# Latent attention: a turn, a spread row and a copy for each head, with the steps of the two heads interleaved

## The chip, the core and the metric

The kernel runs on one core of a Trainium2 chip. The core has TensorE (PE), which multiplies matrices and writes to PSUM; VectorE (DVE) and ScalarE (ACT), which read and write SBUF and PSUM; GpSimd (POOL), which in this kernel adds and multiplies in SBUF; and SyncE (SP), which here issues DMAs. Each has its own queue and takes its instructions in order; they wait for one another through semaphores. The metric is the device time of one execution in microseconds (us); lower is better.

## The reference

The whole reference is a model of two blocks of layers. The change touches one stage of it, the latent attention (MLA) of layer 0. Tokens are 256 of a context and 1024 of the sequence, 1280 in all; there are 8 heads, whose queries and keys have 64 + 32 (rotated) values and whose values have 64.

```python
q = to_heads(rmsnorm(cq, q_norm) @ w_uq, MLA_HEADS)
kv = to_heads(rmsnorm(ckv, kv_norm) @ w_ukv, MLA_HEADS)
...
def block_attention(q, k, v, scale):
    ...
    def one_block(qi):
        s = jnp.einsum('bhqd,bhkd->bhqk', qi, k).astype(jnp.float32) * scale
        p = jax.nn.softmax(s, axis=-1).astype(v.dtype)
        return jnp.einsum('bhqk,bhkd->bhqd', p, v)
...
a_lat = block_attention(qa_l, jnp.concatenate([ka_c, ka_l], axis=2), jnp.concatenate([va_c, va_l], axis=2), scale)
y_ctx = combine(block_attention(qa_c, ka_c, va_c, scale), h_c, mo_c, z_c, u_ctx.dtype)
```

Sequence queries see all 1280 keys, context queries see the 256 keys of the context. Everything is fp32.

## The kernel before

The stage is `mla_block`. Its first part (projections, norms, keys and values) is not touched. The part that the change touches is the attention loop at its end.

**Tiling.** A group is one pair of heads j (0 to 3) and one tile t of 128 query tokens. For each pair there are 8 full groups (t from 2 to 9, 10 tiles of 128 keys each) and then 2 small ones (t = 0 and 1, 2 key tiles each): 40 groups. A unit u is one head of one group, u = 2g + hh, where hh says head 0 or head 1 of the pair. Scores lie transposed: keys on partitions, queries along the row. Head 0 has PSUM banks 0 to 2 (`S[0]`), head 1 has banks 3 to 5 (`S[1]`), bank 6 (`TR`) takes the small transposes, bank 7 (`B7`) takes the queries (columns 256 to 511) and the output with its totals (columns 0 to 255). A matmul of fp32 appears in the trace as two instructions, a transpose as one.

**Steps of a group**, with their lines:

- `up_q` (PE, L991) makes the queries of group g + 2 in B7; `copy_q` (ScalarE, L1189) copies them to one of three buffers; `turn_q` (POOL, L850) multiplies in the rotation.
- `score` (PE, L1006): one matmul for each key tile. It waits for the rotated queries (`q_ev`) and, since the banks are used again, for the subtraction of the same head in the group before (`lowered`).
- `tops` (VectorE, L1289): the maximum over the key tiles, which leaves 128 x 128. `turn_top` (PE, L1012) transposes this. `highest` (VectorE, L1293) reduces the two transposed heads at once to two columns `mx`. `spread_max` (PE, L1017) spreads the two columns over rows by two matmuls with the identity. `copy_max` (ScalarE, L1193) copies both spread rows to `low`.
- `lower` (VectorE, L1299) subtracts the maximum of a head from its scores and writes them to one of four buffers `pr`. `soft` (ScalarE, L1198) takes the exponential in place.
- `key_sums` (POOL, L862, L864 and L867) adds the key tiles of the exponentials: for a full group one addition of 640 columns (L864) and three smaller (L867).
- `weigh` (PE, L1028) multiplies by the values, two heads side by side in the halves of the array. `total_up` (PE, L1034) makes the totals over the keys from the partial sums of POOL.
- `outputs` (VectorE, L1307 and L1309): the reciprocal of the totals and the product, both read from B7. SyncE stores the result (L816).

**What sets the order.** All orders are written out by hand. In each turn g of the loop PE does: turn of head 0, queries of g + 2, turn of head 1, first half of `weigh(g - 1)`, both spreads, second half of `weigh(g - 1)`, `total_up(g - 1)`, scores of head 0 and of head 1 of group g + 1. VectorE does: tops of both heads, `highest` for both, `lower` for both, `outputs(g - 1)`. ScalarE does: `copy_q(g + 2)`, `copy_max(g)`, `soft` for both. POOL does: `turn_q(g + 2)`, then `key_sums` for both heads. Users of B7 take it in order (`take_bank`): after `outputs` for the queries and the next weighing (`oev`), after `copy_q` (`q_raw`).

After the loop comes the matrix-memory (mLSTM) stage, which begins when the block of this stage has ended on all engines. Two of its weight tiles are loaded during the loop (L812).

Of the kernel before, what the change touches and what calls it, by code (L numbers as in the profile page):

```python
# [9 lines left out]
ALU = mybir.AluOpType  # L10
# [692 lines left out]
def mla_block(nc, name, U, H, io, v_dram, a_dram, n_dram, f_dram, o_dram, mod, gain, rcol, mod1, ones, ident, eps, ahead, h_late, w_first):  # L703
# [20 lines left out]
    with Stage(nc, name) as s:  # L724
        area = s.sb("area", [P, 7680 + 5120 + 2560 + 1280 + 6400 + 5120 + 1280])

        def part(o, *dims):
# [19 lines left out]
        top, low = part(V, 2, P), part(V + 2 * P, 2, P)  # L747
# [6 lines left out]
        mx = s.sb("mx", [P, 2, 2])  # L754
# [16 lines left out]
        scored, topped, top_tr, maxed, max_mm, max_row, lowered, exped, partial, pv, oev = (  # L771
            s.sem(c) for c in ("scored", "topped", "top_tr", "maxed", "max_mm", "max_row", "lowered", "exped", "partial", "pv", "oev"))
# [46 lines left out]
        def _(pool):  # L819
# [33 lines left out]
            def key_sums(u):  # L853
# [4 lines left out]
                pool.wait_ge(q_ev, min(2 * g + 6, 2 * NG))  # L858
# [13 lines left out]
            for g in range(NG):  # L872
                if g + 2 < NG:
                    turn_q(g + 2)
                key_sums(2 * g)
                key_sums(2 * g + 1)

        @block.tensor
        def _(pe):
# [116 lines left out]
            def score(u):  # L996
                g, hh = divmod(u, 2)
                j, t = groups[g]
                pe.wait_ge(q_ev, 2 * g + 2)
                if u >= 2:  # L1000
                    pe.wait_ge(lowered, u - 1)
                else:
                    pe.wait_ge(kv_a, kv_act[len(KV)])
                    pe.wait_ge(kv_d, kv_dve[len(KV)])
                for kt in range(nkt[g]):
                    last = nc.tensor.matmul(S[hh][:, kt * P:(kt + 1) * P], k[:, j, hh, kt * P:(kt + 1) * P], q[:, g % 3, hh, :],  # L1006
                                            start=True, stop=True)
                last.then_inc(scored, 1)
# [12 lines left out]
            def weigh(g, tiles):  # L1021
                j, t = groups[g]
                if tiles[0] == 0:
                    take_bank()
                    pe.wait_ge(exped, 2 * g + 2)
                for kt in tiles:
# [3587 lines left out]
```

## Time and profile before

| what | value |
| --- | --- |
| time, median of 3 runs | 4080.45 us (4075.15 to 4082.25) |
| time of the profiled execution | 4078.14 us |
| its span, first to last instruction | 4076.2 us |
| mean granted clock of TensorE | 0.991 |
| attention loop in the span | about 297 to 698 us |

How to read it: the span is cut into stretches by the window view, which gives for each stretch how long each engine was busy, in the order PE (matmuls), PEld (weight loads), DVE, ACT, POOL, and the granted clock, where 1.00 is 2.4 GHz. The timeline gives start and length of instructions in order of time; "x20" says that a row holds 20 of them, merged, and its length is from the start of the first to the end of the last, so that two long instructions in a row share one length. The bracket behind a row is the idle time of the engine before it and what ended it. PE's matmuls overlap one another and their ends are modelled, so PE's place in its list is best read from the starts of the weight loads. "mla_banks" is the PSUM of the stage, "sbuf" is the one SBUF area of the kernel.

### The profile page before, as it was taken

Reading aid. Unit: us, or ns where it says so; the run is one execution under the profiler, and the core shown is the slowest. Engines: PE = TensorE matmul, PEld = TensorE weight load, DVE = VectorE, ACT = ScalarE, POOL = GpSimd, SP = SyncE. Lnnn points to the kernel's source line nnn. Section 1 sums busy time; section 2 is a strip of 40 time slices with the busy share of each in tenths; the row PEclk is TensorE's granted clock in tenths of the full one; section 3 lists DMA queues with packets and bytes.
Section 4 is the critical chain, followed back from the end, with each engine's and each line's share of the span. In section 5 each row is a group of like instructions: output and inputs, shape, how many; then the busy total and the mean of one; then the engine's idle time right before and its main releaser. Section 6 shows DMA issues by size and latency. Waiting matters only on the chain. (4 is left out here: it accounts for less than half of the span.)

```text
span 4076.2 us, 48063 instructions
## 1 busy us (share of the span) xinstructions
PE 3957.3 (97%) x18570; PEld 2449.3 (60%) x18570; DVE 1771.0 (43%) x3730; ACT 941.7 (23%) x1722; POOL 836.9 (21%) x911
## 2 busy tenths in 40 slices
PE   7998888999999999989999999999999999999998
PEld 4687887777558559567544565656544444444447
DVE  3236666577334266746356322222523252223134
ACT  4223322243214411145325311111111000000001
POOL 0006665100111111132013111122200022111222
PEclk9999999999999999989999999999999999999999
DMA  5320001211202111132122112113243111111113
GB/s 211 127 86 7 8 8 32 54 60 40 96 21 86 51 59 57 55 110 79 63 81 63 57 36 79 38 59 101 94 183 106 52 31 41 42 42 50 43 41 104
DMA packets 113569, 270.23 MB, mean 66 GB/s; under 512 B 15479, under 2 KB 45033, under 8 KB 112254
## 3 DMA queue, kind: packets, MB, share of 16 engines
q1 hardware_dynamic: 106368, 251.81, 18.7%
q0 software_dynamic: 5920, 13.25, 1.3%
q8 instruction: 149, 2.44, 0.3%
q10 hardware_dynamic: 1056, 2.10, 0.1%
q14 instruction: 76, 0.62, 0.0%
HBM read 218.53 MB, written 50.87 MB: 66 GB/s over the span
## 5 line engine op out<-in xcount | busy, mean ns | idle before, releaser
L426 PE MATMUL upper_banks<-sbuf 128*128 128x512 f32 (+1 forms) x2016 | 773.0, 546 | 2.6 <-issue 2.2
L3136 PE MATMUL upper_banks<-sbuf 128*128 128x512 f32 x1400 | 614.6, 595 | 6.5 <-ACT sbuf L3395 3.4
L426 PEld LDWEIGHTS upper_banks<-sbuf 128*128 128x128 f32 x2016 | 383.6, 191 | 390.3 <-issue 375.8
L3136 PEld LDWEIGHTS upper_banks<-sbuf 128*128 128x128 f32 x1400 | 262.6, 191 | 317.4 <-issue 307.2
L2401 PE MATMUL gla_prod<-sbuf 128*128 128x512 f32 x560 | 247.6, 593 | 0.3 <-DVE sbuf L2433 0.3
L378 POOL TENSOR_TENSOR sbuf<-sbuf 128x512 f32<-128x512 f32 x36 | 46.5, 1292 | 906.4 <-POOLq L68 331.2
L582 DVE TENSOR_TENSOR sbuf<-upper_banks,sbuf 128x512 f32<-128x512 f32 (+1 forms) x140 | 81.8, 585 | 284.8 <-PE upper_banks L426 284.3
L1006 PE MATMUL mla_banks<-sbuf 128*128 128x128 f32 x1344 | 161.9, 279 | 28.4 <-DVE sbuf L1299 28.4
L1006 PEld LDWEIGHTS mla_banks<-sbuf 128*128 128x128 f32 x1344 | 154.8, 193 | 37.1 <-issue 37.1
L2401 PEld LDWEIGHTS gla_prod<-sbuf 128*128 128x128 f32 x560 | 104.5, 192 | 119.9 <-issue 117.4
L1611 PE MATMUL mls_banks<-sbuf 128*128 128x512 f32 x392 | 175.1, 593 | 0.0
L3636 DVE TENSOR_TENSOR sbuf<-upper_banks,sbuf 128x512 f32<-128x512 f32 x75 | 53.5, 715 | 224.4 <-PE upper_banks L3136 215.2
L1299 DVE TENSOR_TENSOR sbuf<-mla_banks,sbuf 128x1280 f32<-128x1280 f32 (+1 forms) x80 | 98.5, 1273 | 73.9 <-ACT sbuf L1193 73.9
L549 DVE TENSOR_TENSOR sbuf<-upper_banks,sbuf 128x512 f32<-128x512 f32 x48 | 33.1, 691 | 223.0 <-PE upper_banks L426 223.0
L470 ACT ACTIVATE sbuf<-upper_banks 128x512 f32<-128x512 f32 x48 | 28.7, 597 | 429.4 <-PE upper_banks L426 429.4
L864 POOL TENSOR_TENSOR sbuf<-sbuf 128x640 f32<-128x640 f32 x64 | 98.8, 1544 | 92.4 <-ACT sbuf L1198 92.4
L1611 PEld LDWEIGHTS mls_banks<-sbuf 128*128 128x128 f32 x392 | 71.6, 190 | 75.9 <-issue 74.1
L1289 DVE TENSOR_REDUCE sbuf<-mla_banks 128x128 f32<-128x1280 f32 (+1 forms) x80 | 101.5, 1277 | 35.5 <-PE mla_banks L1006 34.9
L3167 PE MATMUL upper_banks<-sbuf 128*128 128x256 f32 (+2 forms) x512 | 115.5, 385 | 1.0 <-DVE sbuf L3781 0.6
L4189 PE MATMUL upper_banks<-sbuf 128*128 128x512 f32 x256 | 112.7, 600 | 0.0
L918 PE MATMUL mla_banks<-sbuf 128*128 128x512 f32 (+1 forms) x288 | 108.0, 533 | 4.7 <-ACT sbuf L1112 4.7
L3377 PE MATMUL upper_banks<-sbuf 128*128 128x512 f32 x256 | 110.6, 592 | 0.0
(534 smaller groups left out, 6489.1 us busy)
## 6 DMA issues: line engine op xcount, KB each, us to landing
sbuf<-in_l_w_in SPq DMA_DIRECT2D x59, 512.0 KB, 4.0
sbuf<-in_w_in SPq DMA_DIRECT2D x52, 512.0 KB, 4.2
sbuf<-in_w_mlp_out SPq DMA_DIRECT2D x40, 512.0 KB, 3.6
sbuf<-in_w_mlp_in SPq DMA_DIRECT2D x32, 512.0 KB, 3.7
sbuf<-in_l_w_mod SPq DMA_DIRECT2D x24, 512.0 KB, 5.1
scratch_gates<-sbuf SPq DMA_DIRECT2D x48, 256.0 KB, 2.0
sbuf<-scratch_gates SPq DMA_DIRECT2D x8, 1536.0 KB, 6.6
sbuf<-in_l_w_mod SPq DMA_DIRECT2D x8, 1024.0 KB, 15.3
```

Of the source, the lines that this page charges most:

```text
L426: last = nc.tensor.matmul(bank_of(n, c)[:, 0:wd], lw[:, k * P:(k + 1) * P], right_operand(c, base, tw, k, o, wd, to), start=k == 0 and c i ...
L864: nc.gpsimd.tensor_tensor(to, e[:, 0:5 * P], e[:, 5 * P:10 * P], ALU.add).then_inc(partial, 1)
L918: last = nc.tensor.matmul(banks[:, bank, 0:wd], wk, U[:, kk, o:o + wd], start=kk == 0, stop=kk == KD - 1)
L1006: last = nc.tensor.matmul(S[hh][:, kt * P:(kt + 1) * P], k[:, j, hh, kt * P:(kt + 1) * P], q[:, g % 3, hh, :], start=True, stop=True)
L1289: nc.vector.reduce_max(top[:, hh, :], S[hh][:, 0:nkt[g] * P].rearrange("p (t q) -> p q t", q=P), AX).then_inc(topped, 1)
L1299: nc.vector.tensor_tensor(pr[:, u % 4, 0:nkt[g] * P].rearrange("p (t q) -> p t q", q=P), S[hh][:, 0:nkt[g] * P].rearrange("p (t q) -> p t ...
L1611: last = nc.tensor.matmul(banks[:, n % 2, :], lw[:, kk * P:(kk + 1) * P], right, start=c in ("P1", "P2", "P5") and kk == 0, stop=kk == 3, ...
L2401: last = nc.tensor.matmul(pb, wk, right, start=fresh and kk == 0, stop=kk == 3, skip_group_check=True)
L3136: last = nc.tensor.matmul(pb, lw[:, k * P:(k + 1) * P], rhs, start=k == 0 and c in ("P1", "P2", "P5"), stop=k == 3, skip_group_check=True)
L3167: last = nc.tensor.matmul(dst, lhsT, rhs, start=k == 0, stop=k == KD - 1)
L3377: last = nc.tensor.matmul(O[:, n % 2, :], w_out[j][:, k * P:(k + 1) * P], U[:, k, NCTX + half * 512:NCTX + half * 512 + 512], start=k == 0 ...
L4189: last = nc.tensor.matmul(banks[:, n % 4, :], w[j][:, kk * P:(kk + 1) * P], x[:, half * 512:half * 512 + 512], start=kk == 0, stop=kk == K ...
```

## The change

Each head now has its own small steps, and the order on all four engines is new.

- `highest`, `spread_max`, `copy_max` work on one unit. `mx` has one column for each head. The spread is one transpose of the column repeated 128 times, no matmul. `TR` is used in columns 0 to 127 for the turned tops and 128 to 255 for the spread row by all units; `turn_top(u)` therefore waits for the copy of the row of unit u - 1 (`max_row`).
- `copy_out(g)` is new: ScalarE copies the output and its totals (256 columns of B7) to one of two SBUF buffers `raw`. `outputs` reads both from there. B7 is free after this copy (`o_raw`) and not after the product (`oev`).
- PE: the scores of a head are cut in two parts, between which another step stands; `weigh` is whole.
- POOL: `turn_q(g + 2)` stands behind the key sums of group g.

The diff, without the lines that only declare semaphores and buffers:

```diff
-        top, low = part(V, 2, P), part(V + 2 * P, 2, P)
+        top, low, raw = part(V, 2, P), part(V + 2 * P, 2, P), part(V + 4 * P, 2, 2 * P)
...
             def turn_q(g):
                 pool.wait_ge(q_raw, g + 1)
-                if g >= 3:
-                    pool.wait_ge(partial, sum(adds[:2 * g - 4]))
+                if g >= 2:
+                    pool.wait_ge(partial, sum(adds[:2 * g - 2]))
...
             for g in range(NG):
+                key_sums(2 * g)
+                key_sums(2 * g + 1)
                 if g + 2 < NG:
                     turn_q(g + 2)
-                key_sums(2 * g)
-                key_sums(2 * g + 1)
...
             def turn_top(u):
                 pe.wait_ge(topped, u + 1)
-                nc.tensor.transpose(TR[:, (u % 2) * P:(u % 2 + 1) * P], top[:, u % 2, :], ident[:]).then_inc(top_tr, 1)
-            def spread_max(g):
-                pe.wait_ge(maxed, g + 1)
-                for hh in range(2):
-                    last = nc.tensor.matmul(TR[:, (2 + hh) * P:(3 + hh) * P], mx[:, g % 2, hh:hh + 1].broadcast_to([P, P]), ident[:],
-                                            start=True, stop=True)
-                last.then_inc(max_mm, 1)
+                if u:
+                    pe.wait_ge(max_row, u)
+                nc.tensor.transpose(TR[:, 0:P], top[:, u % 2, :], ident[:]).then_inc(top_tr, 1)
+            def spread_max(u):
+                pe.wait_ge(maxed, u + 1)
+                nc.tensor.transpose(TR[:, P:2 * P], mx[:, u % 2:u % 2 + 1].broadcast_to([P, P]), ident[:]).then_inc(max_mm, 1)
...
-            score(0)
-            score(1)
-            for g in range(NG + 1):
-                before = range(nkt[g - 1]) if g else ()
-                if g < NG:
-                    turn_top(2 * g)
-                if g + 2 < NG:
-                    up_q(g + 2)
-                if g < NG:
-                    turn_top(2 * g + 1)
-                if g:
-                    weigh(g - 1, before[:len(before) // 2])
-                if g < NG:
-                    spread_max(g)
-                if g:
-                    weigh(g - 1, before[len(before) // 2:])
-                    total_up(g - 1)
-                if g + 1 < NG:
-                    score(2 * g + 2)
-                    score(2 * g + 3)
+            score(0, range(nkt[0]))
+            for g in range(NG):
+                tiles = range(nkt[g])
+                cut = 7 if nkt[g] == TT else 1
+                score(2 * g + 1, tiles[:cut])
+                turn_top(2 * g)
+                score(2 * g + 1, tiles[cut:])
+                spread_max(2 * g)
+                if g:
+                    weigh(g - 1)
+                turn_top(2 * g + 1)
+                if g:
+                    total_up(g - 1)
+                if g + 1 < NG:
+                    after = range(nkt[g + 1])
+                    cut = 3 if nkt[g + 1] == TT else 1
+                    score(2 * g + 2, after[:cut])
+                    spread_max(2 * g + 1)
+                    if g + 2 < NG:
+                        up_q(g + 2)
+                    score(2 * g + 2, after[cut:])
+                else:
+                    spread_max(2 * g + 1)
+            weigh(NG - 1)
+            total_up(NG - 1)
...
+            def copy_max(u):
+                act.wait_ge(max_mm, u + 1)
+                nc.scalar.activation(low[:, u % 2, :], TR[:, P:2 * P], ACT.Copy).then_inc(max_row, 1)
+            def copy_out(g):
+                act.wait_ge(pv, g + 1)
+                if g >= 2:
+                    act.wait_ge(oev, g - 1)
+                nc.scalar.activation(raw[:, g % 2, :], B7[:, 0:2 * P], ACT.Copy).then_inc(o_raw, 1)
...
             for g in range(NG):
+                copy_max(2 * g)
+                if g:
+                    copy_out(g - 1)
+                soft(2 * g)
+                copy_max(2 * g + 1)
                 if g + 2 < NG:
                     copy_q(g + 2)
-                copy_max(g)
-                soft(2 * g)
                 soft(2 * g + 1)
+            copy_out(NG - 1)
...
             for g in range(NG):
                 tops(2 * g)
+                highest(2 * g)
                 tops(2 * g + 1)
-                highest(g)
                 lower(2 * g)
-                lower(2 * g + 1)
+                highest(2 * g + 1)
                 if g:
                     outputs(g - 1)
+                lower(2 * g + 1)
             outputs(NG - 1)
```

`highest(u)` reduces `TR[:, 0:P]` to one column, `lower(u)` waits for `max_row` of its own unit, and `outputs(g)` waits for `o_raw` and takes the reciprocal of `raw[:, g % 2, P:2 * P]` and the product with `raw[:, g % 2, 0:P]`.

## Rows read from the trace of the kernel before

**Rows 1.** Windows: busy us of each engine (instructions), granted clock, DMA share, GB/s.
```profile
297.00:698.00 401.00, 354.75 (x3553) 317.37 (x3551) 262.70 (x279) 119.00 (x160) 245.04 (x351) 0.99 0.03 9
```

**Rows 2.** Waits, 297 to 700 us: who <- for whom: total us, times, longest.
```profile
DVE sbuf L1299 <- ACT sbuf L1193: 73.9, 40, 2.3
...
PE mla_banks L1006 <- DVE sbuf L1299: 28.4, 39, 2.1
```

**Rows 3.** Timeline of a full group: start, us, engine, line, [idle before <-releaser].
```profile
408.11 4.54 PEld L1006 LDWEIGHTS mla_banks<-sbuf 128*128 128x128 f32 x40 [1.72 <-issue]
...
409.31 0.95 DVE L1307 RECIPROCAL sbuf<-mla_banks 128x128 f32<-128x128 f32 x1
409.38 1.56 POOL L864 TENSOR_TENSOR sbuf<-sbuf 128x640 f32<-128x640 f32 x1 [3.54 <-ACT sbuf L1198]
410.33 0.29 DVE L1309 TENSOR_TENSOR sbuf<-mla_banks,sbuf 128x128 f32<-128x128 f32 x1
...
412.57 0.14 PEld L1012 LDWEIGHTS mla_banks<-sbuf 128*128 128x128 f32 x1
...
412.68 1.42 PEld L991 LDWEIGHTS mla_banks<-sbuf 128*128 128x128 f32 x12
412.76 1.54 POOL L864 TENSOR_TENSOR sbuf<-sbuf 128x640 f32<-128x640 f32 x1
...
412.88 1.49 DVE L1289 TENSOR_REDUCE sbuf<-mla_banks 128x128 f32<-128x1280 f32 x1 [0.74 <-PE mla_banks L1006]
...
414.43 0.14 PEld L1012 LDWEIGHTS mla_banks<-sbuf 128*128 128x128 f32 x1 [0.33 <-DVE sbuf L1289]
...
414.76 1.07 PEld L1028 LDWEIGHTS mla_banks<-sbuf 128*64 128x64 f32 x20 [0.20 <-ACT sbuf L1189]
...
414.79 0.43 DVE L1293 TENSOR_REDUCE sbuf<-mla_banks 128x2 f32<-128x256 f32 x1 [0.42 <-PE mla_banks L1012]
416.01 0.52 PEld L1017 LDWEIGHTS mla_banks<-sbuf 128*128 128x128 f32 x4 [0.17 <-issue]
...
416.31 0.99 POOL L850 TENSOR_TENSOR sbuf<-sbuf 64x128 f32<-64x128 f32 x2
416.65 1.07 PEld L1028 LDWEIGHTS mla_banks<-sbuf 128*64 128x64 f32 x20
...
416.76 0.38 ACT L1193 ACTIVATE sbuf<-mla_banks 128x256 f32<-128x256 f32 x1 [2.04 <-PE mla_banks L1017]
417.17 2.89 DVE L1299 TENSOR_TENSOR sbuf<-mla_banks,sbuf 128x1280 f32<-128x1280 f32 x2 [1.95 <-ACT sbuf L1193]
417.68 0.25 PEld L1034 LDWEIGHTS mla_banks<-sbuf 128*64 128x64 f32 x4
...
418.70 1.27 ACT L1198 ACTIVATE sbuf<-sbuf 128x1280 f32<-128x1280 f32 x1 [1.56 <-DVE sbuf L1299]
418.78 0.41 PEld L1006 LDWEIGHTS mla_banks<-sbuf 128*128 128x128 f32 x3 [0.84 <-issue]
```

**Rows 4.** Timeline: score loads at the two small groups of a pair.
```profile
383.65 0.52 PEld L1006 LDWEIGHTS mla_banks<-sbuf 128*128 128x128 f32 x4 [0.84 <-issue]
...
392.13 0.97 PEld L1006 LDWEIGHTS mla_banks<-sbuf 128*128 128x128 f32 x8 [0.17 <-issue]
...
398.18 3.98 PEld L1006 LDWEIGHTS mla_banks<-sbuf 128*128 128x128 f32 x35 [0.65 <-issue]
```

**Rows 5.** Groups by line and form, 297 to 698 us: busy us, mean ns.
```profile
L1289 DVE TENSOR_REDUCE sbuf<-mla_banks 128x128 f32<-128x256 f32 x16 | 6.0, 415 | 0.0
```

**Rows 6.** Timeline of the MLP block: additions of VectorE and POOL, all from SBUF.
```profile
3333.43 0.69 DVE L542 TENSOR_TENSOR sbuf<-sbuf 128x512 f32<-128x512 f32 x1
...
3337.21 1.60 POOL L380 TENSOR_TENSOR sbuf<-sbuf 128x512 f32<-128x512 f32 x1
...
3337.78 1.58 DVE L542 TENSOR_TENSOR sbuf<-sbuf 128x512 f32<-128x512 f32 x1
...
3338.77 1.71 POOL L381 TENSOR_TENSOR sbuf<-sbuf 128x512 f32<-128x512 f32 x1
```

More of the change, by code:

```diff
@@ L753, in mla_block @@
         gq, gk = s.sb("gq", [P, 3]), s.sb("gk", [P, 2])
[L754 removed]
+        mx = s.sb("mx", [P, 2])
         banks = s.ps("banks", [P, 8, 512])
@@ L770, in mla_block @@
         q_mm, q_raw, q_ev = (s.sem(c) for c in ("q_mm", "q_raw", "q_ev"))
-        scored, topped, top_tr, maxed, max_mm, max_row, lowered, exped, partial, pv, oev = (
-            s.sem(c) for c in ("scored", "topped", "top_tr", "maxed", "max_mm", "max_row", "lowered", "exped", "partial", "pv", "oev"))
+        scored, topped, top_tr, maxed, max_mm, max_row, lowered, exped, partial, pv, o_raw, oev = (
+            s.sem(c) for c in ("scored", "topped", "top_tr", "maxed", "max_mm", "max_row", "lowered", "exped", "partial", "pv", "o_raw", "oev"))
         o_out = [s.sem(f"o_out{i}") for i in range(4)]
@@ L994, in up_q, with score @@
                 used[0] = (q_raw, g + 1)
-            def score(u):
+            def score(u, tiles):
                 g, hh = divmod(u, 2)
                 j, t = groups[g]
[L999 to L1005, printed above, removed]
+                if tiles[0] == 0:
+                    pe.wait_ge(q_ev, 2 * g + 2)
+                    if u >= 2:
+                        pe.wait_ge(lowered, u - 1)
+                    else:
+                        pe.wait_ge(kv_a, kv_act[len(KV)])
+                        pe.wait_ge(kv_d, kv_dve[len(KV)])
+                for kt in tiles:
@@ L1006, in score @@
                     last = nc.tensor.matmul(S[hh][:, kt * P:(kt + 1) * P], k[:, j, hh, kt * P:(kt + 1) * P], q[:, g % 3, hh, :],
                                             start=True, stop=True)
-                last.then_inc(scored, 1)
+                if tiles[-1] == nkt[g] - 1:
+                    last.then_inc(scored, 1)
             def turn_top(u):
                 pe.wait_ge(topped, u + 1)
-                nc.tensor.transpose(TR[:, (u % 2) * P:(u % 2 + 1) * P], top[:, u % 2, :], ident[:]).then_inc(top_tr, 1)
@@ L1022, in weigh @@
+            def spread_max(u):
+                pe.wait_ge(maxed, u + 1)
+                nc.tensor.transpose(TR[:, P:2 * P], mx[:, u % 2:u % 2 + 1].broadcast_to([P, P]), ident[:]).then_inc(max_mm, 1)
+            def weigh(g):
                 j, t = groups[g]
[L1023 to L1026, printed above, removed]
+                take_bank()
+                pe.wait_ge(exped, 2 * g + 2)
+                for kt in range(nkt[g]):
@@ L1036, in total_up @@
                 last.then_inc(pv, 1)
-                used[0] = (oev, g + 1)
+                used[0] = (o_raw, g + 1)
             pe.wait_ge(wm_in, 48)
@@ L1131, in _ @@
                 if n == 1:
-                    nc.scalar.activation(mx[:, 0, 0:1], eps, ACT.Sqrt)
+                    nc.scalar.activation(mx[:, 0:1], eps, ACT.Sqrt)
                     act.wait_ge(hsum, 1)
@@ L1303, in outputs @@
             def outputs(g):
-                dve.wait_ge(pv, g + 1)
+                dve.wait_ge(o_raw, g + 1)
                 if g >= 4:
                     dve.wait_ge(o_out[g % 4], 16 * (g // 4))
-                nc.vector.reciprocal(stage[:, g % 4, :], B7[:, P:2 * P])
+                nc.vector.reciprocal(stage[:, g % 4, :], raw[:, g % 2, P:2 * P])
                 dve.drain()
-                nc.vector.tensor_tensor(stage[:, g % 4, :], B7[:, 0:P], stage[:, g % 4, :], ALU.mult).then_inc(oev, 1)
+                nc.vector.tensor_tensor(stage[:, g % 4, :], raw[:, g % 2, 0:P], stage[:, g % 4, :], ALU.mult).then_inc(oev, 1)
             b, (o, wd) = 1, thirds()[1]
```

15 lines of the change are left out of this document (6 added, 9 removed).

## The prediction

> **What bounds the kernel now.** Times are in microseconds (us). The window view comes first: in the attention loop (297 to 698 us, 401 of the 4076.2 us span) TensorE (PE) is busy 354.8, VectorE (DVE) 262.7, POOL 245.0, at a granted clock of 0.99 [rows 1]. So no engine is full, and every one waits for another; the PE still idles about a tenth. The waits say for whom: the subtraction of L1299 waits 73.9 us in 40 times for ScalarE's (ACT) copy of the maxima, and the next scores wait 28.4 us in 39 times for L1299 [rows 2]. That is a ring, and the timeline of one full group shows it whole [rows 3]. I read PE's position from its weight loads, since the matmuls' ends are modelled.
>
> The ring, from score load to score load, 408.11 to 418.78: 40 score loads, 4.46; 0.31 to the start of the second head's maximum; 1.49 for it; 0.06 to its turn; 1.58 until the spread's loads start (turn, 0.22 for a copied q, half of the weighing); 0.75 until the copy; 0.41 until L1299; 1.49 for the first subtraction; 0.12 back to PE. Sum 10.67, the period [rows 3]. In it PE waits 0.41 (414.02 to 414.43), 0.22 (414.54 to 414.76) and 0.68 (418.10 to 418.78), 1.31 in all; what PE needs is 9.36. The small groups go outside this: score load to score load takes 8.48 (383.65 to 392.13) for the first, 6.05 (to 398.18) for the second [rows 4]. Ten groups, one pair of heads, take 8 x 10.67 + 14.5 = 99.9, four times.
>
> **The change part by part.** Slots of PE [rows 3]: 0.1115 per load of 128 columns (4.46/40), two loads per matmul, so 7 tiles 1.56, 3 tiles 0.67, q 1.34 (12 loads); a turn has one load, 0.11; a weighing load 0.0535 (1.07/20), plus about 0.1 on entering 64-column tiles (416.53 to 416.65) and 0.17 on leaving (415.83 to 416.01).
>
> - *Spreads by transposing.* Two matmuls of two loads each (0.64 with the change of tiles) become two turns of 0.11, since a transposition has one load where a matmul has two. PE's need falls to 4.46 + 4 x 0.11 + 1.34 + (0.1 + 2.14 + 0.17) + (0.1 + 0.21 + 0.17) = 9.13.
> - *Smaller VectorE and ScalarE steps.* One reduction of 256 columns (0.43) becomes two of 128. No row has that; bounds are 0.14 (a third) and 0.43; by L1309's 0.29 for 128 columns I take 0.29. ScalarE's 256-column copy (0.38) becomes two of 128: between 0.19 and 0.38, I take 0.26. Both are per head and within the waits below.
> - *Values copied out.* A further 0.38 on ScalarE, priced by L1193. The reciprocal (0.95) and product (0.29) are taken at their lengths of before; with inputs in SBUF the reciprocal lies between 0.29 (the product's, same columns) and 1.49 (L1289), the product between 0.29 and 1.85 (below). A shorter reciprocal gives nothing, since the row of head 1 comes later; at 1.49 the period gains 0.05.
>
> Now the new order. Clock 0 is the first load of head 1's scores. Head 0's maximum starts at 0.31, ends 1.80; its turn starts 1.86 where PE stands ready at 1.56, **wait 0.30**. The small maximum starts 0.36 after a turn (414.43 to 414.79): 2.22 to 2.51. PE does the last 3 tiles to 2.64, the spread to 2.75, and the weighing to 5.16. VectorE: head 1's maximum 2.95 to 4.44, then the subtraction of head 0, whose row was copied by about 3.3, to 5.92. PE turns head 1's maximum at 5.16 and makes the totals 5.37 to 5.75; the next scores of head 0 need 5.92 + 0.12 = 6.04, **wait 0.29**. 3 tiles, the spread and q take PE to 8.16, 7 tiles to 9.72. Meanwhile ScalarE copies out at about 5.86 to 6.24 (0.49 after the totals start), raises head 0 to exponentials until 7.54, copies head 1's row until 7.80; VectorE has head 1's small maximum at 5.95 to 6.24, reciprocal and product 6.27 to 7.58, the subtraction of head 1 at 7.83 to 9.31. The next group's start needs 9.43, PE is there at 9.72: **0.29 to spare**. So the period is 9.13 + 0.30 + 0.29, with rounding **9.73** against 10.67, 0.94 less.
>
> The waits that move: the turn of a head now also waits for the other head's copied row (about 3.3 against 5.16, free). Copying out waits for the totals, and the exponentials stand behind it in ScalarE's queue. q's copy on ScalarE comes at 8.5 to 8.9, ahead of head 1's exponentials (9.4), so nothing waits for it. SyncE's stores (L816) wait for the product as before, which comes 2 us later in the turn, and have three more buffers. q's rope on POOL is moved behind both key sums. POOL: from the exponentials' end 7.54, two key sums of 3.38 (409.38 to 412.76), rope 0.98, so 15.4; less a period 5.7, with the hop 5.8, where scores want it at 6.04. 0.2 to spare. As a ring over two periods (3.68 from head 0's scores to the next clock 0, 7.54 to the exponentials' end, 7.9 to the rope, 0.1) it is 19.2, a floor of 9.6 per group: POOL is the next bound, close below. ScalarE's ring (key sum end, totals, copy out, exponentials, two key sums) is 0.1 + 0.49 + 0.38 + 1.30 + 6.8 = 9.1, with hops.
>
> Small groups, walked likewise, with a reduction of 415 ns [rows 5]: the last full turn is cut by head 1's subtraction at 9.43. The first small one waits with its totals for POOL's key sums of the last full group until 5.0, then for rope until 6.0, and with one tile, spread, q and one tile more (1.9) lasts 7.9. In the second PE is through its totals at 2.9, rope is there at 2.5, and 10 tiles, spread and q of the next full group add 3.7: 6.6. A pair of heads is 7 x 9.73 + 9.43 + 7.9 + 6.6 = 92.0 against 99.9, four times 31.6. The first group's start has nothing to weigh and gains less: before it took 10 where others took 10.67, afterwards VectorE holds it at 9.7, minus 0.7. The tail gets one copy (0.4) and loses about as much. What follows, the matrix-memory stage, starts with weights already loaded, so its end moves by the same: 31 us. The profiled execution took 4078.14, span 4076.2; it lies 2.3 below the median of 4080.45. Predicted: 4078 - 31 = 4047.
>
> **A rule of the chip against it.** The product at L1309 now reads both inputs from SBUF. Where two such instructions meet in this trace, they exclude each other: a VectorE addition of 0.69 took 1.58 when issued 0.57 into a POOL addition (1.03 to the POOL one's end, then 0.55), and the POOL one issued next took 1.71 [rows 6]. The product of before, one input in PSUM, took its 0.29 in the middle of POOL's L864 [rows 3]. In the new order the product starts 1.05 after the copy-out ends (reciprocal 0.95, drain), and POOL's first sum starts 1.38 after it (0.03 + 1.27 exponentials, 0.05 to 0.08 hop): the product comes first by 0.33 and ends just as POOL starts.
> The Trainium skill, SBUF — State Buffer, Who interferes with whom, says it as a rule: a VectorE instruction with two SBUF inputs contends with a GpSimd one that reads SBUF, and whichever issued first holds the pair throughout. By that rule the trace agrees, and at worst the second waits for the whole of the first.
>
> **The rivals.**
> - *A, the product loses the race* (slower than before). If head 1's small maximum ends more than 0.33 after the copy-out, the product is issued behind L864 and waits for its end: product ends at 1.38 + 1.56 + 0.29 after 6.24, at 9.45; head 1's subtraction ends 10.95, PE starts at 11.07 in place of 9.73. Eight full turns of 10 pay about 1.35: 92.0 + 10.8 = 102.8 per pair against 99.9, so 12 slower, 4090. For it: rows 6, and that both times hang on estimates of 0.1. Against: the two chains start from one event. Chance 0.07.
> - *B, POOL binds.* Its margins of 0.2 and the floor of 9.6 hang on hops. Were key sums or the hop to copying out 0.5 later per group, scores wait for rope, the period is about 10.1 to 10.2, and the gain 4 x 8 x 0.4 = 13 less: 4060. For it: POOL would be at 7.7 of 9.7, with two queues ahead of it. Against: L864 takes 1.54 to 1.56 with VectorE at work beside it [rows 3]. Chance 0.18.
> - *C, no gain:* the interleaving costs what it saves, as each turn makes PE wait in order with all behind it; the waits for copies come back as 0.9 per group. 4078. Against: a turn inside a stream costs 0.11 now (412.57 to 412.68). Chance 0.05.
>
> **How the numbers follow.** The forecast has 0.70. Its own range: period 9.6 (floor) to 9.95 (the maximum and copy at their upper bounds, a hop more in each wait), with the small groups 1 either way per pair: 4039 to 4058. The range adds B and reaches towards C: 4037 to 4068. What a measurement can tell from no change here is 0.2%, 8 us. Faster: the forecast, B and little else, 0.88; same 0.05; slower 0.07.
>
> **What would show it.** Right: score start to score start of full groups at 9.7; PE's waits of 0.3 before the turn of head 0 and 0.3 before head 0's next scores, none on POOL; L1309 at 0.29; the stage about 370 long; later stages shifted and unchanged. Wrong: L1309 above 1 us with a period of 11 (A); scores waiting for L850 or the totals waiting for L867 in full groups (B); turns preceded by more than 0.5 (C). The forecast fails if the period is above 10 or a later stage changes its length.

## The result and the profile after

The kernel after the change takes 4052.5 us (median, 4050.4 to 4058.0) where the one before takes 4080.9 in the same comparison: ratio 0.9934, 95% interval 0.9921 to 0.9948, so 28 us less. Forecast: 4047, range 4037 to 4068. The profiled execution took 4052.3, span 4050.5.

The change moves the line numbers of the stage: score loads L1007, turn L1016, spread L1020, weighing L1028, totals L1034; maxima L1304, small maximum L1308, subtraction L1314, reciprocal L1322, product L1324; ScalarE copies the row at L1198, values at L1204, q at L1194, and makes exponentials at L1209. POOL's lines are those of before.

The window view over the loop, columns as in [rows 1]:

```profile
301.00:674.00 373.00, 345.74 (x3473) 307.38 (x3471) 269.60 (x320) 133.63 (x240) 245.61 (x351) 0.98 0.03 10
```

PE's idle time falls from 46.2 to 27.3 and its busy time from 354.8 to 345.7 [rows 1]: two thirds of the gain are waits that went, one third is work, though the granted clock of the stretch is a little lower (0.98 against 0.99). From the first score load to the end of the last product the loop took 400.8 before and takes 372.5: 28.3 less, as much as the difference of the medians.

The timeline of one full group, from head 0's scores to the next ones, answers to [rows 3]:

```profile
401.18 0.74 PEld L1007 LDWEIGHTS mla_banks<-sbuf 128*128 128x128 f32 x6 [1.00 <-issue]
...
410.76 0.74 PEld L1007 LDWEIGHTS mla_banks<-sbuf 128*128 128x128 f32 x6 [0.21 <-issue]
...
410.83 0.38 ACT L1204 ACTIVATE sbuf<-mla_banks 128x256 f32<-128x256 f32 x1 [2.70 <-PE mla_banks L1034]
411.12 1.26 ACT L1209 ACTIVATE sbuf<-sbuf 128x1280 f32<-128x1280 f32 x1
411.25 0.95 DVE L1322 RECIPROCAL sbuf<-sbuf 128x128 f32<-128x128 f32 x1 [0.41 <-ACT sbuf L1204]
411.42 0.14 PEld L1020 LDWEIGHTS mla_banks<-sbuf 128*128 128x128 f32 x1
...
411.53 1.42 PEld L991 LDWEIGHTS mla_banks<-sbuf 128*128 128x128 f32 x12
...
412.28 0.29 DVE L1324 TENSOR_TENSOR sbuf<-sbuf 128x128 f32<-128x128 f32 x1
412.46 1.55 POOL L864 TENSOR_TENSOR sbuf<-sbuf 128x640 f32<-128x640 f32 x1 [2.08 <-ACT sbuf L1209]
412.58 1.49 DVE L1314 TENSOR_TENSOR sbuf<-mla_banks,sbuf 128x1280 f32<-128x1280 f32 x1
412.87 3.21 PEld L1007 LDWEIGHTS mla_banks<-sbuf 128*128 128x128 f32 x28
...
414.74 1.49 DVE L1304 TENSOR_REDUCE sbuf<-mla_banks 128x128 f32<-128x1280 f32 x1 [0.67 <-PE mla_banks L1007]
...
416.29 0.14 PEld L1016 LDWEIGHTS mla_banks<-sbuf 128*128 128x128 f32 x1 [0.21 <-DVE sbuf L1304]
...
416.29 0.80 PEld L1007 LDWEIGHTS mla_banks<-sbuf 128*128 128x128 f32 x6
...
416.65 0.29 DVE L1308 TENSOR_REDUCE sbuf<-mla_banks 128x1 f32<-128x128 f32 x1 [0.42 <-PE mla_banks L1016]
417.01 0.14 PEld L1020 LDWEIGHTS mla_banks<-sbuf 128*128 128x128 f32 x1
...
417.32 2.16 PEld L1028 LDWEIGHTS mla_banks<-sbuf 128*64 128x64 f32 x40 [0.17 <-issue]
...
418.73 1.48 DVE L1314 TENSOR_TENSOR sbuf<-mla_banks,sbuf 128x1280 f32<-128x1280 f32 x1
419.39 0.99 POOL L850 TENSOR_TENSOR sbuf<-sbuf 64x128 f32<-64x128 f32 x2
419.66 0.14 PEld L1016 LDWEIGHTS mla_banks<-sbuf 128*128 128x128 f32 x1 [0.17 <-issue]
...
420.43 0.74 PEld L1007 LDWEIGHTS mla_banks<-sbuf 128*128 128x128 f32 x6 [0.31 <-POOL sbuf L850]
```

PE waits at two places only: at the turn of head 0 (0.21) and briefly ahead of head 0's scores; the other brackets of 0.17 are those on leaving 64-column tiles. The group lasts 9.67 (410.76 to 420.43), and POOL ends it: the subtraction is done at 420.21, the rotation of q (L850, called the rope below) at 420.38. The group before it lasted 9.58 (401.18 to 410.76); there the subtraction was done last (409.16 and 1.48 are 410.64) and the rope 0.26 earlier. So it goes on, 9.57 and 9.66 in turn, mean 9.62. From head 0's scores (401.18) to the rope that the scores two groups later wait for (420.38) it is 19.20: a ring over two groups, with the hop to PE 19.24 long. The period was 10.67.

The waits of the loop (total us, times, longest) answer to [rows 2]:

```profile
POOL sbuf L864 <- ACT sbuf L1209: 74.9, 32, 7.6
...
PEld mla_banks L1016 <- DVE sbuf L1304: 13.2, 39, 1.7
...
PEld mla_banks L1007 <- POOL sbuf L850: 10.2, 28, 0.9
...
PE mla_banks L1007 <- DVE sbuf L1314: 8.5, 9, 1.2
...
PEld mla_banks L1034 <- POOL sbuf L867: 5.2, 4, 1.3
...
DVE sbuf L1314 <- ACT sbuf L1198: 4.2, 9, 1.3
```

The subtraction's wait for the copied row went from 73.9 to 4.2, the scores' wait for the subtraction from 28.4 to 8.5 [rows 2]. New are waits for POOL: for the rotated q (L850) at 28 score starts, and for the key sums (L867) at four totals, one in each pair of heads. The latter are at the small groups, of which these lines show one (before: [rows 4]):

```profile
385.64 0.20 PEld L1034 LDWEIGHTS mla_banks<-sbuf 128*64 128x64 f32 x4 [1.29 <-POOL sbuf L867]
...
386.75 0.30 PEld L1007 LDWEIGHTS mla_banks<-sbuf 128*128 128x128 f32 x2 [0.92 <-POOL sbuf L850]
```

### The profile page after: what moved, and what is told of

It is laid out like the page before. It is cut to its first block and busy times, and to the rows that moved or that the text cites. A ratio compares the mean times of both kernels' runs of the same rounds, so it can differ in the third digit from the quotient of the medians.

```text
span 4050.5 us, 48141 instructions
## 1 busy us (share of the span) xinstructions
PE 3951.8 (98%) x18490; PEld 2440.7 (60%) x18490; DVE 1775.2 (44%) x3770; ACT 957.0 (24%) x1802; POOL 835.2 (21%) x911
## 5 line engine op out<-in xcount | busy, mean ns | idle before, releaser
L1007 PE MATMUL mla_banks<-sbuf 128*128 128x128 f32 x1344 | 175.2, 279 | 12.1 <-DVE sbuf L1314 8.5
L1007 PEld LDWEIGHTS mla_banks<-sbuf 128*128 128x128 f32 x1344 | 162.7, 194 | 21.8 <-issue 11.6
L1304 DVE TENSOR_REDUCE sbuf<-mla_banks 128x128 f32<-128x1280 f32 (+1 forms) x80 | 102.2, 1278 | 48.5 <-PE mla_banks L1007 48.4
L867 POOL TENSOR_TENSOR sbuf<-sbuf 128x128 f32<-128x128 f32 (+1 forms) x192 | 105.2, 548 | 15.1
```

The costliest lines, as they stand in the source:

```text
L867: nc.gpsimd.tensor_tensor(to[:, 0:w0], to[:, 0:w0], to[:, o:o + w0], ALU.add).then_inc(partial, 1)
L1304: nc.vector.reduce_max(top[:, hh, :], S[hh][:, 0:nkt[g] * P].rearrange("p (t q) -> p q t", q=P), AX).then_inc(topped, 1)
```

## The experiments

The reciprocal stands once in each group, so the intervals between its starts give the period of full groups and the three intervals behind the last full group; in the kernel after these three are 8.95, 5.60, 9.04, and the next is 10.07. Without a fall of the clock the ten intervals of a pair of heads sum to 91.38. A ratio is to the kernel before, with its 95% interval.

**Spreads by transposing, alone (the kernel before with this one edit).**
```diff
-                    last = nc.tensor.matmul(TR[:, (2 + hh) * P:(3 + hh) * P], mx[:, g % 2, hh:hh + 1].broadcast_to([P, P]), ident[:],
-                                            start=True, stop=True)
+                    last = nc.tensor.transpose(TR[:, (2 + hh) * P:(3 + hh) * P], mx[:, g % 2, hh:hh + 1].broadcast_to([P, P]), ident[:])
```


> The kernel before with one edit: the two spreads of a group are transposes (one load each) and not matmuls (two loads each). Ring theory (the period is the sum of the steps that release one another around TensorE and VectorE): the ring of before holds the spread from its first load to the copy, 0.75 us; with two loads in place of four it is 0.5 to 0.55, so the period falls from 10.67 to about 10.45, and with 40 groups the time by 8 to 10 us, to about 4071. Rival (work theory: TensorE idles in this stage anyway, so less work on it gives nothing): 4080.


Measured: 4070.9, ratio 0.9980 (0.9970 to 0.9989), period 10.39. As expected: the cheaper spread alone is worth 0.28 a group and 9 us, so it lay in the ring.

**Head 1's scores uncut (after, the turn behind all ten tiles).**
```diff
-                cut = 7 if nkt[g] == TT else 1
+                cut = nkt[g]
                 score(2 * g + 1, tiles[:cut])
                 turn_top(2 * g)
-                score(2 * g + 1, tiles[cut:])
```


> The changed kernel with the scores of head 1 in one piece of 10 tiles, the turn of head 0 behind them (it was cut after 7). Ring theory: the wait before the turn goes, but VectorE does head 0's small maximum 0.37 us later and head 1's maximum starts at the same time or up to 0.1 earlier, so the period stays at 9.6 and the time at 4052, within 3 us. Rival (interleaving as such pays: a turn behind 3 more tiles delays all that hangs on it by 0.4 us): period 9.9 to 10.0, 4064.


Measured: 4061.5, ratio 0.9955 (0.9939 to 0.9970), period 9.89. The ring theory's 9.6 and 4052 were wrong, the rival's 9.9 and 4064 near. The timeline of this kernel shows the price:

```profile
410.10 0.14 PEld L1016 LDWEIGHTS mla_banks<-sbuf 128*128 128x128 f32 x1
...
410.52 0.29 DVE L1307 TENSOR_REDUCE sbuf<-mla_banks 128x1 f32<-128x128 f32 x1 [0.85 <-PE mla_banks L1016]
...
410.86 0.13 PEld L1020 LDWEIGHTS mla_banks<-sbuf 128*128 128x128 f32 x1 [0.62 <-DVE sbuf L1307]
```

A turn and its spread are a round trip of 0.76 through VectorE (0.42 and 0.29, then 0.05 back). PE idles 0.62 of it where nothing stands between them; in the kernel after the last three tiles do. The turn's own wait (0.30, see below) goes, so the net is 0.3 a group, and 0.27 is measured: PE has next to no slack to pay it from.

**Head 0's next scores uncut (after, head 1's spread and q behind them).**
```diff
-                    cut = 3 if nkt[g + 1] == TT else 1
-                    score(2 * g + 2, after[:cut])
+                    score(2 * g + 2, after)
                     spread_max(2 * g + 1)
                     if g + 2 < NG:
                         up_q(g + 2)
-                    score(2 * g + 2, after[cut:])
```


> The changed kernel with the scores of head 0 of the next group in one piece, spread of head 1 and queries behind them (it was cut after 3). Ring theory: the spread of head 1 comes 1.56 us later, its subtraction about 1.1 later, past the 0.3 to spare, so TensorE waits about 0.8 per full group at the next group's start: period 10.3 to 10.4, time 4075 to 4080. Rival (where the spread stands doesn't matter as long as TensorE has work in front of the wait): 4052.


Measured: 4070.4, ratio 0.9978 (0.9968 to 0.9987), period 10.41. The period is as expected, the time 5 below the expected range: a full group pays 0.79, but the intervals at the small groups pay nothing together (8.93, 5.09, 9.03), so a pair of heads takes 96.2 in place of 91.4, 19 in all. Head 1's row comes late, its subtraction waits for the copy, and the next scores for the subtraction:

```profile
410.29 1.49 DVE L1312 TENSOR_TENSOR sbuf<-mla_banks,sbuf 128x1280 f32<-128x1280 f32 x1 [1.65 <-ACT sbuf L1196]
...
411.90 1.64 PEld L1007 LDWEIGHTS mla_banks<-sbuf 128*128 128x128 f32 x14 [0.81 <-issue]
```

**Values not copied out (after, VectorE reads them in PSUM as before).**
```diff
-                used[0] = (o_raw, g + 1)
+                used[0] = (oev, g + 1)
...
-                if g:
-                    copy_out(g - 1)
...
-            copy_out(NG - 1)
...
-                dve.wait_ge(o_raw, g + 1)
+                dve.wait_ge(pv, g + 1)
...
-                nc.vector.reciprocal(stage[:, g % 4, :], raw[:, g % 2, P:2 * P])
+                nc.vector.reciprocal(stage[:, g % 4, :], B7[:, P:2 * P])
...
-                nc.vector.tensor_tensor(stage[:, g % 4, :], raw[:, g % 2, 0:P], stage[:, g % 4, :], ALU.mult).then_inc(oev, 1)
+                nc.vector.tensor_tensor(stage[:, g % 4, :], B7[:, 0:P], stage[:, g % 4, :], ALU.mult).then_inc(oev, 1)
```


> The changed kernel without the copy of the values by ScalarE: VectorE reads output and totals from PSUM as before, and the bank is free only after its product. Ring theory: the queries of group g + 2 then wait for the product (about 1.35 us after the totals are there) where they now wait for a 0.38 us copy: 0.6 to 0.8 later on TensorE's path, period 10.2 to 10.4, 4072 to 4078. Rival (the copy is only a further step for ScalarE, since nothing waited for the bank before): 4052 or a little less, as ScalarE gets head 0's exponentials done 0.4 earlier and POOL's rope with them.


Measured: 4071.6, ratio 0.9982 (0.9972 to 0.9991), period 10.25, both as expected (the time at the lower edge). Its waits show that q's loads wait for the product, until which the bank that q needs isn't free:

```profile
PEld mla_banks L991 <- DVE sbuf L1321: 25.1, 37, 1.1
```

That is 0.68 each, against 0.63 of period: ScalarE's 0.38 is off the path, the bank's release is on it.

**POOL's order of before (after, q's rope ahead of the key sums).**
```diff
-                if g >= 2:
-                    pool.wait_ge(partial, sum(adds[:2 * g - 2]))
+                if g >= 3:
+                    pool.wait_ge(partial, sum(adds[:2 * g - 4]))
...
-                pool.wait_ge(q_ev, min(2 * g + 4, 2 * NG))
+                pool.wait_ge(q_ev, min(2 * g + 6, 2 * NG))
...
+                if g + 2 < NG:
+                    turn_q(g + 2)
                 key_sums(2 * g)
                 key_sums(2 * g + 1)
-                if g + 2 < NG:
-                    turn_q(g + 2)
```


> The changed kernel with POOL's order of before: the rope of group g + 2 ahead of the key sums of group g, with the waits that belong to it. Ring theory: the rope waits for the copied queries, which now come 2.4 us after head 0's scores begin, so both key sums start 2.6 later, the totals wait for them, and the ring totals, scores, queries, copy, rope, two key sums, totals closes at 0.1 + 0.4 + 2.4 + 0.4 + 1.0 + 6.8 = 11.1: period 11.1, 4098 to 4105, slower than the kernel before. Rival (POOL has room, its order doesn't matter: 7.7 of 9.6 us busy): 4052.


Measured: 4124.8, ratio 1.0113 (1.0092 to 1.0133). Slower than before, as expected, but by 44 and not by 17 to 24. The totals wait for key sums, because the rope in front of them waits for q's copy:

```profile
429.60 0.20 PEld L1034 LDWEIGHTS mla_banks<-sbuf 128*64 128x64 f32 x4 [1.79 <-POOL sbuf L867]
...
432.86 0.99 POOL L850 TENSOR_TENSOR sbuf<-sbuf 64x128 f32<-64x128 f32 x2 [3.31 <-ACT sbuf L1194]
```

The periods mostly alternate between 11.2, which is the expected ring, and 12.3 to 12.9. Into each of the longer ones falls a short slice at the granted clock of 0.5. There are 19 slices in the loop ahead of its tail, one of them twice as long, where before has one at its start and then its tail. At 1.5 each, and the long one as two, they make some 30 us (an estimate from the intervals), and 4125 less 30 is 4095, just below the expected 4098 to 4105. The expectation left out the clock. No run separates what the waits cost by themselves from what the clock that fell with them costs.

**The reciprocal taken twice (after).**
```diff
+                for _ in range(2):
-                nc.vector.reciprocal(stage[:, g % 4, :], raw[:, g % 2, P:2 * P])
-                dve.drain()
+                    nc.vector.reciprocal(stage[:, g % 4, :], raw[:, g % 2, P:2 * P])
+                    dve.drain()
```


> The changed kernel with the reciprocal taken twice, so that the product comes 1.0 us later, after POOL's first key sum has begun. Theory of exclusion (a VectorE product with two SBUF inputs and a POOL addition shut each other out): the product is issued about 0.75 into POOL's addition of 1.55, waits for its end and lasts 0.9 to 1.1 in place of 0.29; the subtraction of head 1 is then 1.5 late against the 0.3 to spare, period 10.8 to 11.1. Rival (no exclusion, only the added reciprocal): the product keeps 0.29, period 10.2 to 10.3.


Measured: 4083.2, ratio 1.0006 (0.9995 to 1.0016), period 10.55. The product is now issued inside POOL's addition:

```profile
430.46 1.54 POOL L864 TENSOR_TENSOR sbuf<-sbuf 128x640 f32<-128x640 f32 x1 [1.56 <-ACT sbuf L1209]
...
431.32 0.84 DVE L1325 TENSOR_TENSOR sbuf<-sbuf 128x128 f32<-128x128 f32 x1
...
432.08 1.48 DVE L1314 TENSOR_TENSOR sbuf<-mla_banks,sbuf 128x1280 f32<-128x1280 f32 x1
...
433.67 0.41 PEld L1007 LDWEIGHTS mla_banks<-sbuf 128*128 128x128 f32 x3 [0.96 <-issue]
```

The product takes 0.84 in place of 0.29 and ends 0.16 after POOL's addition. The exclusion is there, but the period is between the two theories. Head 1's subtraction starts 3.23 after the copy-out (428.85 to 432.08) where it was 1.75 (410.83 to 412.58), so it is 1.48 late, the 1.5 of the theory. Of this 0.24 was to spare, where the theory had 0.3. What the theory left out comes behind it: since head 0's scores are done long before PE resumes at 433.67, head 0's turn doesn't wait any more, which gives 0.25 back (from there to the next totals 5.24 in place of 5.49). That leaves 0.99, and from 9.57 to 10.55 is 0.98.

**Exponentials ahead of the copy-out (after): rival A in its place.**
```diff
+                soft(2 * g)
                 if g:
                     copy_out(g - 1)
-                soft(2 * g)
```


> After, with ScalarE making head 0's exponentials before it copies the values out. Theory (the product and POOL's L864 exclude each other, and the order of the two chains on ScalarE decides which comes first: rival A of the prediction, in its place): POOL starts 0.38 earlier, the reciprocal about 1.3 later, so the product is issued within L864 and takes 0.3 to 0.6 in place of 0.29; head 1's subtraction starts 1.2 to 1.4 later, of which 0.3 or less was to spare, so PE waits about 1 at the start of each group and the period is 10.5 to 10.8: 4080 to 4090. Rival (nothing in the order matters since POOL's ring is the bound and it starts 0.38 earlier): period 9.4 to 9.6, 4045 to 4052.


Measured: 4072.4, ratio 0.9981 (0.9971 to 0.9992), period 10.30. The direction is the first theory's, the size smaller. POOL's addition, q's loads and the product of one group:

```profile
414.93 1.53 POOL L864 TENSOR_TENSOR sbuf<-sbuf 128x640 f32<-128x640 f32 x1 [1.30 <-ACT sbuf L1209]
...
415.18 1.41 PEld L991 LDWEIGHTS mla_banks<-sbuf 128*128 128x128 f32 x12 [0.69 <-ACT sbuf L1204]
...
416.19 0.43 DVE L1324 TENSOR_TENSOR sbuf<-sbuf 128x128 f32<-128x128 f32 x1
```

The product loses the race and ends again 0.16 after POOL's addition, but it is only 0.14 longer; the reciprocal's start is late, 1.48 after head 0's score start (413.68) where it was 0.49. The new order has a second effect, which the expectation left out: the bank comes free later too, and q's loads wait 0.69 for the copy-out. They start 1.50 after head 0's scores where it was 0.77 (410.76 to 411.53), and this 0.73 alone is as much as the period grew (10.30 against 9.57 or 9.62). By its own work PE would be at head 1's scores at 418.07; the subtraction, done at 418.02, releases them at 418.13. So the 20 us are the price of the order, by two paths within 0.06 of each other, and what the product's 0.14 adds to the period is 0.06 at most.

**Spreads as matmuls (after).**
```diff
-                nc.tensor.transpose(TR[:, P:2 * P], mx[:, u % 2:u % 2 + 1].broadcast_to([P, P]), ident[:]).then_inc(max_mm, 1)
+                nc.tensor.matmul(TR[:, P:2 * P], mx[:, u % 2:u % 2 + 1].broadcast_to([P, P]), ident[:], start=True, stop=True).then_inc(max_mm, 1)
```


> The changed kernel with the two spreads as matmuls (two loads each) again. Ring theory: the first spread is off the ring (TensorE has 0.2 to spare before head 0's scores), the second is on it: 0.11 to 0.2 more per full group, but POOL's ring of two periods (9.62) covers up to 0.05 of it: period 9.7 to 9.8, 4055 to 4058. Rival (the gain of the change is mostly TensorE's shorter spreads, as the run that did them alone gave 9 of its 28 us): 4061.


Measured: 4061.7, ratio 0.9956 (0.9940 to 0.9973), period 9.76. The period is the ring theory's, the time is above its 4055 to 4058 and at the rival's 4061. So the transposed spread is worth 0.14 a group here, half of what it was in the old order. A pair of heads without a fall of the clock takes 92.8 against 91.4, 6 in all; in time it is 9 us. The profiled execution (4064.7) has three more falls of the clock in the loop, some 5 us (11.92 twice where 10.30 is usual, 7.50 for 5.88). That the edit brings them isn't shown, so the last 3 us, and with them the rival, stay open.

**POOL's last addition left to TensorE (after, the totals accumulate two partial sums of each head).**
```diff
-    adds = [4 if nkt[g] == TT else 1 for g in range(NG) for hh in range(2)]
+    adds = [3 if nkt[g] == TT else 1 for g in range(NG) for hh in range(2)]
-                for n, (w0, o) in enumerate(((2 * P, 2 * P), (P, P), (P, 4 * P))):
+                for n, (w0, o) in enumerate(((2 * P, 2 * P), (P, P))):
...
-                for hh in range(2):
-                    last = nc.tensor.matmul(B7[64 * hh:64 * hh + 64, P:2 * P], ones[:, 0:64], part_sum[:, (2 * g + hh) % 4, 0:P],
-                                            start=True, stop=True)
+                parts = (0, 4) if nkt[g] == TT else (0,)
+                for a in parts:
+                    for hh in range(2):
+                        last = nc.tensor.matmul(B7[64 * hh:64 * hh + 64, P:2 * P], ones[:, 0:64], part_sum[:, (2 * g + hh) % 4, a * P:(a + 1) * P],
+                                                start=a == 0, stop=a == parts[-1])
```


> The changed kernel with the last of POOL's four additions of a full key sum left to TensorE: the totals of a head are two matmuls that accumulate. POOL has 0.91 less per group, TensorE 0.21 more, before a wait of about 0.2. Ring theory: POOL's ring of two periods falls from 19.24 to 18.3 and no longer binds, so the alternation of 9.57 and 9.66 goes and all full groups take 9.57; at the small groups the totals and the rope wait 0.9 to 1.8 less, and the clock has less reason to fall: together 5 to 8 us, 4045 to 4048. Rival (TensorE binds, its added loads cost as much as the waits give): 4052 to 4056.


Measured: 4052.8, ratio 0.9936 (0.9921 to 0.9951): no different from after, as the rival had it. The full groups went to 9.75, without alternation, and the small intervals to 8.25, 5.38, 9.04, 10.29. The timeline shows eight loads for the totals and PE busy up to the scores, with the 0.17 of the tiles alone:

```profile
426.20 0.42 PEld L1036 LDWEIGHTS mla_banks<-sbuf 128*64 128x64 f32 x8
426.79 0.74 PEld L1007 LDWEIGHTS mla_banks<-sbuf 128*128 128x128 f32 x6 [0.17 <-issue]
```

The ring theory failed on the size of PE's slack ahead of head 0's scores: it is below 0.1 where 0.2 was taken, and 0.21 more of loads costs 0.13 a group. POOL's relief is worth 0.7 and 0.2 at the small groups. The two cancel.

**The same in one full group of each ten, the last before the small ones (after).**
```diff
-    adds = [4 if nkt[g] == TT else 1 for g in range(NG) for hh in range(2)]
+    adds = [(3 if g % 10 == 7 else 4) if nkt[g] == TT else 1 for g in range(NG) for hh in range(2)]
...
+                parts = (0, 4) if g % 10 == 7 else (0,)
```


> After, with POOL's last addition left to TensorE's accumulating totals in one full group of each ten alone, the last before the small ones. In after the interval behind that group is 8.95 where leaving all groups' last additions to TensorE gave 8.25, and the following ones were 5.60 against 5.38; the full groups keep 9.57/9.66. Theory (the small groups wait for POOL's queue, the full groups for POOL's ring and TensorE alike): intervals 9.57/9.66 in full groups, 8.25 to 8.4 and 5.4 to 5.6 behind them, 0.7 to 0.9 less for each pair of heads, 3 to 4 in all, and up to 2 more if the clock fall at 480 us does not come: 4047 to 4050. Rival (what is won there is waited for at the next full group, as the 10.29 in place of 10.07 in the kernel without any last addition suggests): 0.3 per pair, 4051 to 4052.


Measured: 4049.1 (4045.8 to 4050.8), ratio 0.9926 (0.9913 to 0.9940), intervals 9.57 and 9.66 in full groups, then 8.24, 5.38, 9.04, 10.07. The wait of the totals at the small group is down from 1.29 to 0.39:

```profile
381.93 0.42 PEld L1036 LDWEIGHTS mla_banks<-sbuf 128*64 128x64 f32 x8 [0.39 <-POOL sbuf L867]
...
383.05 0.30 PEld L1007 LDWEIGHTS mla_banks<-sbuf 128*128 128x128 f32 x2 [0.70 <-POOL sbuf L850]
```

The intervals are those of the first theory: 0.93 less per pair of heads, 3.7 in all. The medians differ by 3.4, and the two intervals of the ratio overlap, so the gain over the change is shown by the rows alone.

## Why the prediction came out as it did

The forecast was 4047, the measured time is 4052.5: the gain is 28 where 31 was forecast, by the mechanism that was walked, except that POOL's ring, which was to come next, already binds. In part the nearness is luck: misses cancel in the pair of heads and between the start and the tail, as told below.

*The small steps.* Right. The small maximum takes 0.288 (estimate 0.29), the row's copy 0.274 (0.26), the copy-out 0.385 (0.38), the reciprocal 0.952 and the product 0.292 (mean), as these rows of the groups by line and form (busy us, mean ns) say:

```profile
L1322 DVE RECIPROCAL sbuf<-sbuf 128x128 f32<-128x128 f32 x40 | 38.1, 952 | 23.2 <-ACT sbuf L1204 23.2
...
L1308 DVE TENSOR_REDUCE sbuf<-mla_banks 128x1 f32<-128x128 f32 x80 | 23.0, 288 | 26.1 <-PE mla_banks L1016 25.8
...
L1198 ACT ACTIVATE sbuf<-mla_banks 128x128 f32<-128x128 f32 x80 | 22.0, 274 | 84.8 <-PE mla_banks L1020 84.8
...
L1324 DVE TENSOR_TENSOR sbuf<-sbuf 128x128 f32<-128x128 f32 x40 | 11.7, 292 | 3.0
```

*The period.* Predicted 9.73 by two waits of 0.30 and 0.29; measured 9.62. With clock 0 at 414.43 (the seven tiles' slots, 1.56, after 412.87), the turn comes at 1.86 as walked, 0.30 after PE stands ready, and the second turn at 5.23 (walked 5.16). The wait that was mis-sized is the second, ahead of head 0's next scores: head 0's subtraction starts at 4.30, not 4.44, because head 1's maximum starts 0.06 earlier and the subtraction starts 0.08 before the maximum's end. So of 0.29 there is left under 0.1, and what the prediction had as the next bound binds: POOL's two-period ring, walked at 19.2, measured 19.24. "None on POOL" was wrong, at a price of 0.05 a group (9.62 against the 9.57 of the groups that POOL doesn't end): rival B's mechanism at a tenth of its size. That POOL's ring sets the mean is read from the rows; no run relieves POOL in the full groups without giving PE work in return. The kernel with head 1's scores uncut and the one with the additions on TensorE show the third bound, PE itself, as near: anything over 0.1 more for PE there is paid.

*The interleaving.* Right: uncutting either head's scores costs 0.27 or 0.79 a group. The copy-out, costed at nothing but ScalarE's 0.38, is what keeps the bank free in time: without it 0.63. The prediction did not name that gain. q's rope behind the key sums is worth more than all the gain of the change: without it the kernel is slower than before, though by the estimate above some 30 of its 72 us go with the clock.

*Rival A.* The product came first by 0.18 (412.28 against 412.46), where 0.33 was walked, and its length was never above 0.30. The rival's price was reckoned as 1.35 a group. No run has the product issued just behind the start of POOL's addition, which that price supposes; the two that come near lost 0.93 (the reciprocal taken twice; of the delay of 1.48 the exclusion is 0.55) and 0.7 (exponentials first, for the order more than for the exclusion). The Trainium skill (SBUF — State Buffer, Who interferes with whom) has a VectorE instruction with two SBUF inputs contend with a GpSimd one that reads SBUF, and whichever issues first hold the shared ports for its whole length. The two kernels that provoke it agree: the product ends 0.16 after POOL's addition. The other way round the hold doesn't show to its very end: in the kernel after, POOL's addition starts 0.11 before the product's end and takes 1.55, hardly more than elsewhere (mean 1.543).

*A pair of heads.* I took 99.9 for before, 8 full groups of 10.67 and 14.5. The reciprocals give 99.16 (7 times 10.67, then 7.40, 6.06, 11.00): the group after the small ones is shorter, 398.18 to 408.11 being 9.93 [rows 3, 4]. The new pair was walked at 92.0 and is 91.38, both short by nearly the same, so the gain is 7.8 a pair against 7.9.

*From 31 to 28.* Four times 7.78 is 31.1. Of it 1.7 goes to one fall of the clock in the loop (479 to 482 us, 7.12 in place of 5.60, and 0.2 elsewhere), and 1.1 to the ends: the start gains 5.0, the last three intervals lose 4.6, where I had put "even", and the four intervals around the small groups (35.1 before, 33.7 after), which bring 1.5 of each pair's 7.78, don't come in the last pair (5.0 less 4.6 less 1.5 is -1.1). The start's 5.0 are 1.8 in the first turn, 2.5 in the second (1.4 of it a slice at half clock that before had there) and 0.7 for the reciprocal's earlier place in the turn. The first turn was mis-sized: from head 0's first scores to its next ones it took 9.9 before (297.63 to 307.57) and takes 8.1 (301.67 to 309.80), where 9.7 was walked. The windows show the granted clock of the kernel after ahead of the fall, during it, and in the tail:

```profile
470.00:478.30 8.30, 5.24 (x61) 4.12 (x59) 3.80 (x9) 3.00 (x7) 7.21 (x10) 1.00 0.03 8
478.30:484.70 6.40, 6.04 (x37) 5.06 (x37) 3.17 (x8) 1.33 (x5) 1.82 (x4) 0.73 0.05 13
...
663.00:680.00 17.00, 11.63 (x48) 8.38 (x47) 10.59 (x34) 2.63 (x8) 4.90 (x5) 0.50 0.16 26
```

PE was busy 5.2 of the 8.3 ahead of the fall, with its longest waits for VectorE and POOL; then the twelve loads of q took 2.62 in place of 1.42. The tail has 17 us at 1.2 GHz where before has 6.8; how much of the 4.6 that explains isn't shown.

*The profiled execution* is 25.8 faster and not 28.4: its loop began 4.0 later, because its start was at a lower clock. Windows of the first 60 us, of before, of after, and of the first experiment, which has the code of before there:

```profile
0.00:60.00 60.00, 36.43 (x184) 17.99 (x184) 25.14 (x46) 28.16 (x52) 5.36 (x13) 0.91 0.83 304
```
```profile
0.00:60.00 60.00, 38.88 (x146) 19.17 (x147) 24.63 (x44) 25.57 (x47) 5.36 (x13) 0.80 0.82 304
```
```profile
0.00:60.00 60.00, 38.97 (x146) 19.19 (x147) 24.64 (x44) 25.55 (x47) 5.34 (x13) 0.80 0.82 304
```

The third, 0.80 like the second, shows that the change isn't the cause. Behind the loop the two profiled executions differ by 1.5, so the later stages moved along as predicted.

## What to carry to other kernels

Walk the new order with a clock for every engine, and write down how much each engine has to spare at each meeting point: here three bounds came out within some 0.1 of each other, and the edit that relieved one of them in every group (POOL) gained nothing, since it loaded the next (PE). Copying a result out of a shared PSUM bank pays by the time at which the bank comes free, even if the copying engine adds work. Where groups of two sizes alternate, take the period over a whole cycle from one repeated instruction, not as full groups plus small ones, and look at the change of size for itself: there the same edit took off 0.93 a cycle by the rows.

## What the runs showed of the hardware

- The granted clock fell to 0.5 (1.2 GHz) after stretches in which PE kept waiting for short times: at 479 us in the kernel after, where no wait of PE in the two groups before was above 1.3; and with POOL's order of before in about every other group, with waits of 1.8. One such slice costs 1.5 to 1.7 (12.7 against 11.2; 7.12 against 5.60). Whether a given small group meets one changes between kernels and within one: of three alike in the kernel after, one did. What decides between them stays open.
- A transposition against the identity takes one load slot, 0.11, inside a stream of fp32 matmuls, where a matmul of the same size takes two.
- A VectorE product with both inputs in SBUF, issued within a POOL addition, ended 0.15 to 0.16 after it in the two kernels that provoke it, whether issued 0.86 or 1.26 into it; the 0.69 addition of [rows 6] ended 0.55 after. In all three the VectorE instruction ended behind POOL's by its own length less 0.14. The product of the kernel before, with one input in PSUM, took its 0.29 within a POOL addition in all 31 cases.
- The reciprocal of 128 x 128 takes 0.95 from PSUM and from SBUF alike, the product of the same size 0.29.
